# A streaming encoder step on one core: the projection stage gets its tokens already turned, and forms its halves between two chunks

## The reference, cut to what matters

```
h    = rmsnorm(x, ln1_g)                  # x: (tokens, 1024)
proj = h @ w_in                           # 1024 -> 3080 columns
xc   = causal_conv(x_lru, ..., lru_cw) + lru_cb     # 4 taps, out += xp[j:j+L] * w[j]
hs   = rglru(xc, ...);  out_a = hs * gelu(y_lru)
qkv_c = silu(causal_conv(qkv, ..., gdn_cw))
beta = sigmoid(b_logit);  g = -exp(alog) * softplus(a_logit + dtb)
```

## Time and profile before

| | |
|---|---|
| median of 3 runs | 3766.71 us (3763.04 to 3767.36) |
| the profiled execution's own time | 3768.46 us |
| its span, first to last instruction | 3766.8 us |
| TensorE busy over the span | 85% |
| VectorE busy | 57% |
| ScalarE busy | 41% |
| GpSimd busy | 22% |
| first matmul of group 0 / of the last group | 22.79 us / 1357.97 us |

### The profile page before, as it was taken

How to read it: one execution, slowest core, us unless ns; L and a number is a source line. 1 busy time by engine, 2 the same in 40 slices (tenths; PEclk the granted TensorE clock), 3 DMA queues, 4 the chain that set the end, 5 groups by cost and what they waited for, 6 DMA issues and landing times. The chain is left out here.

```text
span 3766.8 us, 66113 instructions
## 1 busy us (share of the span) xinstructions
PE 3191.2 (85%) x18658; PEld 1938.3 (51%) x18659; DVE 2155.4 (57%) x5335; ACT 1538.5 (41%) x3032; POOL 823.0 (22%) x1002
## 2 busy tenths in 40 slices
PE   8997979788797976699999999998499999999920
PEld 3443434333343456577777777766355555555500
DVE  6574757566665764477677777766433333333358
ACT  6464656556555662233333333332122222222222
POOL 0000000000000001255445554553111111111145
PEclk9998989899898985799999999999799999999965
DMA  4456656574747534445554455433367778985378
GB/s 144 142 182 224 213 194 231 184 258 164 274 159 243 190 127 144 121 138 148 145 146 129 130 145 149 131 112 92 132 223 252 269 266 283 324 295 185 110 275 333
DMA packets 487498, 716.00 MB, mean 190 GB/s; under 512 B 92272, under 2 KB 241360, under 8 KB 486992
## 3 DMA queue, kind: packets, MB, share of 16 engines
q1 hardware_dynamic: 404096, 480.63, 41.3%
q10 hardware_dynamic: 54288, 146.56, 9.8%
q0 software_dynamic: 28864, 86.09, 6.3%
HBM read 442.22 MB, written 270.92 MB: 189 GB/s over the span
## 5 line engine op out<-in xcount | busy, mean ns | idle before, releaser
L338 PE MATMUL pP<-h_hi,w_hi 128*128 128x512 f16 (+1 forms) x1728 | 639.0, 374 | 86.1 <-ACT win L430 67.1
L338 PE MATMUL pP<-h_lo,w_hi 128*128 128x512 f16 (+1 forms) x1728 | 637.6, 373 | 0.0
L338 PE MATMUL pP<-h_hi,w_lo 128*128 128x512 f16 (+1 forms) x1728 | 635.9, 372 | 0.0
L1863 PE MATMUL ebank<-w_halves,rowsT_hi 128*128 x1568 | 485.4, 381 | 1.5 <-ACT rowsT_hi L1899 0.9
L529 DVE SCALAR_TENSOR_TENSOR halves<-stage,halves 128x512 f16<-128x512 f32 x384 | 254.6, 687 | 200.6 <-ACT halves L400 200.4
L400 ACT ACTIVATE halves<-stage 128x512 f16<-128x512 f32 x384 | 236.4, 625 | 273.7 <-DMA stage<-in_raw 264.4
L569 DVE SCALAR_TENSOR_TENSOR cv<-win,cols_sb,cv 128x512 f32<-128x512 f32 (+1 forms) x432 | 305.5, 707 | 35.8 <-issue 1.4
L338 PEld LDWEIGHTS pP<-h_hi,w_hi 128*128 128x128 f16 x1728 | 174.6, 101 | 293.1 <-ACT win L430 80.4
L1863 PE MATMUL ebank<-w_halves,rowsT_lo 128*128 x784 | 298.9, 381 | 0.0
L298 POOL TENSOR_TENSOR ss<-ss,eps 128x4 f32<-128x4 f32 (+1 forms) x9 | 2.2, 249 | 1295.7 <-ACT junk L386 1295.7
L338 PEld LDWEIGHTS pP<-h_hi,w_lo 128*128 128x128 f16 x1728 | 175.1, 101 | 191.7 <-issue 18.3
(11 more groups left out here) (344 smaller groups left out, 6666.9 us busy)
## 6 DMA issues: line engine op xcount, KB each, us to landing
stage<-in_raw SPq DMA_DIRECT2D x384, 256.0 KB, 4.0
split<-halves SPq DMA_DIRECT2D x384, 256.0 KB, 3.3
w_halves<-split SPq DMA_DIRECT2D x32, 2048.0 KB, 11.6
y<-yb ACTq DMA_DIRECT2D x98, 512.0 KB, 7.4
ft<-mixin SPq DMA_DIRECT2D x33, 1280.0 KB, 8.5
mixin<-qo ACTq DMA_DIRECT2D x128, 256.0 KB, 3.7
w_halves<-split SPq DMA_DIRECT2D x32, 1024.0 KB, 6.1
xt<-in_x SPq DMA_DIRECT2D x33, 512.0 KB, 5.2
```

Source lines behind the costliest of these rows:

```text
L338: ins = nc.tensor.matmul(pP[n % NPB][:, 0:N], w[:, k, c0:c0 + P], h[:, k, 0:N], start=(k + i == 0), stop=(k == KD - 1 and i == 2))
L1863: ins = nc.tensor.matmul((M0, M1)[p][:, :], x[p][:, k, :], w[:, bass.ds(s, 1), k, half, :].rearrange("p a n -> p (a n)"), start=(k + i == ...
```

## The change

The tokens are also given with rows and columns exchanged (`xT`). SP loads eight blocks of 128 x 512 of it during the first chunks of the group before (steps "W"), 2 KB in a row; no transposes are left. The token tiles themselves are still loaded, for the sum of squares only, into `gy` (two at a time), and the four passes over them are spread over four steps "N". VectorE forms a diagonal of the inverse norms ("D"), TensorE spreads them over all partitions by one float32 matmul with ones ("E", behind chunk Q8), VectorE scales each block in place ("H", in the Z part), and ahead of Z3 ScalarE writes `h_hi` and VectorE `h_lo` of the next group ("T"), each block k as soon as Z3's matmuls have read it. The first chunk of a group waits for each block apart. The oldest convolution tap on VectorE goes; instead ScalarE writes the newest tap straight from the bank into `cv` by a second activation. There are four banks `pP` instead of three, and seven raw buffers instead of four; `carry_s` and `hl_s` now lie in `stage` and are loaded behind the last piece. `asq` and `amax` share other tiles.

```diff
-NRAW, NHALF = 4, 4
+NRAW, NHALF = 7, 4
...
     for m in range(3, QC):
-        out += [("Q", m)] + p() + [("S", m - 1)] + [("N", 0)] * (m == 6) + [("B", 0)] * (m == 9) + p(2)
-    out += [("Z", 0)] + p() + [("S", QC - 1)] + p(3) + [("Z", 1)] + p(4) + [("Z", 2)] + p(3) + [("Z", 3)] + p()
+        out += [("Q", m)] + p() + [("S", m - 1)] + [("N", m - 2)] * (m < 6) + [("D", 0)] * (m == 7) + [("E", 0)] * (m == 8)
+        out += [("B", 0)] * (m == 9) + p(2)
+    out += [("Z", 0)] + p(2) + [("S", QC - 1)] + p(3) + [("Z", 1)] + [("H", k) for k in range(4)] + p(3)
+    out += [("H", k) for k in range(4, KD)] + [("Z", 2)] + p(3) + [("T", k) for k in range(KD)] + [("Z", 3)] + p()
...
-    NPB = 3
+    NPB = 4
...
+            def spread(g, nt):
+                pe.wait_ge(*norm_did.at("D", g))
+                pe.wait_ge(*norm_did.at(f"H{KD - 1}", g, back=1))
+                nc.tensor.matmul(pR[:, 0:nt * P], ones[:, :], rg[:, 0:nt * P], start=True, stop=True
+                                 ).then_inc(*spread_did.did("E"))
...
-                        ins = nc.tensor.transpose(turned[k % 4][:, t * P:(t + 1) * P], xt[:, t, k * P:(k + 1) * P], ident)
-                    ins.then_inc(*pe_did.did(f"T{k}"))
-                pe.wait_ge(*dve_did.at(f"L{KD - 1}", g))
...
                         for k in range(KD):
+                            if n == 0:
+                                pe.wait_ge(*h_did.at(f"L{k}", g))
...
+            def high(k, g, nt):
+                act.wait_ge(*norm_did.at(f"H{k}", g))
+                act.wait_ge(*pe_did.at(f"{last}.{k}", g, back=1))
+                nc.scalar.activation(h_hi[:, k, 0:nt * P], xT[:, k, 0:nt * P], ACT.Copy).then_inc(*hi_did.did(f"T{k}"))
...
+                        nc.scalar.activation(window(c, 3, stream), shaped(made, stream), ACT.Copy, scale=PROJ)
+                        if 4 <= c < 8:
+                            act.wait_ge(*pe_did.at(f"G{c - 4}", g))
+                        nc.scalar.activation(cv[:, c % 4, 0:N], made, ACT.Identity, scale=col("cw", 4 * c + 3),
+                                             bias=col("cb", m) if kind == "X" else 0.0).then_inc(*act_did.did(f"{kind}{m}"))
...
+            def diagonal(g, nt):
                 dve.wait_ge(*rs_did.at("rs", g))
...
+            def scaled(k, g, nt):
...
+                nc.vector.scalar_tensor_tensor(xT[:, k, 0:N], xT[:, k, 0:N], ln16[:, k:k + 1], pR[:, 0:N],
+                                               ALU.mult, ALU.mult).then_inc(*norm_did.did(f"H{k}"))
...
-                        if kind == "X":
-                            nc.vector.tensor_scalar(dst, window(c, 0, stream), cw(0), col("cb", m), ALU.mult, ALU.add)
-                        else:
-                            nc.vector.tensor_scalar(dst, window(c, 0, stream), cw(0), None, ALU.mult)
                         nc.vector.tensor_copy(kept[:, c], new)
-                        for j in range(1, 4):
+                        for j in (2, 1, 0):
```

More of the change, by code:

```diff
@@ L243, in _ @@
                 if n == 6:
-                    load(1, GT)
+                    for k in range(KD):
+                        turned_load(k, 1, GT)
+                if 14 <= n < 14 + GT:
+                    token_load(n - 14, 1)
                 if n >= 2:
@@ L250, in raw, with group @@
                              ).then_inc(raw_in[i % NRAW], 16)
[L252 to L258, removed]
+            def group(g, base, count, following, n):
+                for kind, i in seq:
+                    if kind == "P" and i < count:
+                        sp.wait_ge(lo_done, base + i + 1)
+                        sp.dma_start(T["split"][bass.ds(base + i, 1)].rearrange("a p b n -> p (a b) n"),
+                                     halves[i % NHALF][:, :, :]).then_inc(halves_out[i % NHALF], 16)
+                        if i < following:
+                            raw(base + i + NRAW, i)
+                    elif kind == "W":
+                        turned_load(i, g + 1, n)
+                    elif kind == "R" and i == LC - 1:
+                        for t in range(min(2, n)):
+                            token_load(t, g + 1)
+                    elif kind == "N" and i + 2 < n:
+                        token_load(i + 2, g + 1)
             sp.wait_ge(w_split, len(wblocks))
@@ L262, in _ @@
                 raw(i, i)
[L263 to L266, removed]
+            with sp.Fori(1, groups - 1) as g:
+                group(g, (g - 1) * PER_GROUP, PER_GROUP, PER_GROUP, GT)
             rest = NE * PIECES - (groups - 2) * PER_GROUP
-            pieces((groups - 2) * PER_GROUP, rest, rest - NRAW)
+            group(groups - 1, (groups - 2) * PER_GROUP, rest, rest - NRAW, 1)
+            sp.dma_start(carry_s, T["conv_s"]).then_inc(states_in, 16)
+            sp.dma_start(hl_s, T["h_s"]).then_inc(states_in, 16)
             for n in range(NHALF):
@@ L360, in group @@
                         ins.then_inc(*pe_did.did("B0"))
[L362 to L365, removed]
+            spread(0, GT)
+            group(0, GT, GT, first=True)
+            with pe.Fori(1, groups - 1) as g:
+                group(g, GT, GT)
+            group(groups - 1, GT, 1)
+            group(groups, 1, 0)
         def shaped(ap, stream):
@@ L479, in _ @@
                 act.sem_inc(s, 16)
-            norm(0, GT)
-            act.wait_ge(setup_in, 16 * 4)
+            for t in range(GT):
+                act.drain()
+                act.wait_ge(first_in, 16 * GT)
+                norm(t, first_tiles[t], 0)
+            act.wait_ge(setup_in, 16 * 2)
             nc.scalar.activation(sp4[:, :], col("lam", 0, LC), ACT.Exp, scale=-1.0)
@@ L494, in _ @@
             act.drain()
+            newest = col("cw", 0, 4 * CC).rearrange("p (c j) -> p c j", j=4)[:, :, 3]
+            nc.scalar.activation(newest, newest, ACT.Copy, scale=PROJ)
+            act.drain()
             nc.scalar.copy(carry[:, 0, 0:1], sp4[:, 0:1]).then_inc(params, 1)
             split(0)
+            for k in range(KD):
+                high(k, 0, GT)
             split(1)
@@ L533, in group @@
                 N = nt * P
[L534 to L537, removed]
                 kept = carry_s if stream else carry
@@ L541, in group @@
                         split(block_of[kind, m] + 2)
-                    if kind == "N" and following:
-                        norm(g + 1, following)
+                    if kind == "D" and following:
+                        diagonal(g + 1, following)
+                    elif kind == "H" and following:
+                        scaled(m, g + 1, following)
+                    elif kind == "T" and following:
+                        low(m, g + 1, following)
                     elif kind == "P" and m < pieces:
@@ L621, in _ @@
             split(0)
+            for k in range(KD):
+                low(k, 0, GT)
             split(1)
```

172 lines of the change are left out of this document (95 added, 77 removed).

## The result

The changed kernel takes 3681.27 us (median of 4 runs, 3671.11 to 3684.69) against 3767.03 for the kernel before in the same runs: ratio 0.9769, 95% interval 0.9749 to 0.979. It is 85.8 us faster, where 148 were forecast (3619). The profiled execution took 3681.03 us, with a span of 3679.4.

What follows compares the result with a forecast made beforehand. The prediction took the Q and Z part as limited by latency first, then transfers. Six groups of 22.6 us plus 14 made 149.6 less than 3768.5, so 3619; own range 3585 to 3655 (0.55), 8 in 10 3550 to 3692.

Steps and rivals of the forecast that it cites:

- The boundary: Between groups: TensorE's 25.1 us to the next chunk would become about 1.3 if ScalarE and VectorE are in time.
- The Q and Z part: Behind chunk Q2 of each full group: 72 us of transfers (25.1 MB at 0.35 MB/us), plus 10 us of remaining stalls.
- I leave half, 10 us: Q and Z part: of 19 us per group above transfers and norm's stop, 10 stay, from the ring of four halves.
- seven buffers remove what is load latency: Q and Z part: seven raw buffers remove the load latency among 19 us per group; the ring of four halves stays.
- 2 us lost out of the 10: Behind chunk Q8: TensorE waits up to 16 us for VectorE's diagonal, but only 2 us per group are lost.
- seven loads can land meanwhile: At step B, where ScalarE stops for its tables and VectorE waits 4.9 us: seven raw loads can land during the stop.
- The norm's stop: Step N: ScalarE's four passes, GpSimd's power and VectorE's scaling stop the pieces about 9.5 us per group; this goes wholly.
- Group 7: The group with 48 pieces: 148.95 us to about 140, -9, from its boundary and waits behind `win`.
- I take nothing: Work shifted between engines: ScalarE 98 to 107 us per group, VectorE 110 to 106; counted as no effect, bounds -3 and +4.
- the halves ring: Rival, chance 0.21: four halves buffers and stores behind loads keep nearly the old pace; 162 us per group, 3692.
- TensorE's pace: Rival, chance 0.17: lateness vanishes and TensorE sets the pace; groups take 137 to 141 us, time 3549.
- Stores behind loads: Rival, chance 0.04: on SP's shared queue stores land in 7.5 us or more instead of 3.3; slower, 3826.

Runs made afterwards that it cites:

- experiment 10: The changed kernel, but the first chunk of a group waits for the last lo half instead of for each block; 3708.39 us, ratio 0.9865 to the kernel before.
- experiment 4: The changed kernel with six pieces per group moved forward, behind Y0, X0 and Y1 instead of behind Q6 to Q11; 3646.81 us.
- experiment 1: The changed kernel with four raw buffers instead of seven, halves staying at four; 3693.82 us.
- experiment 3: The changed kernel with step E behind chunk Q11 instead of behind Q8; 3646.80 us.
- experiment 7: The changed kernel with E behind Q11, six pieces per group moved forward, and step B behind Y1 instead of behind Q9; 3583.18 us.
- experiment 12: The kernel before, with VectorE's share of the norm two chunks later, behind Q8, ScalarE's passes unmoved; 3746.64 us, ratio 0.9962.
- experiment 6: The changed kernel with the convolution as before: four taps on VectorE, one evacuation on ScalarE; 3673.48 us, ratio 0.9768 to the kernel before.
- experiment 11: The changed kernel with three banks instead of four for the chunks; 3669.37 us, ratio 0.9765 to the kernel before.
- experiment 2: The changed kernel with four raw buffers and seven halves instead of seven and four; 3692.13 us.
- 8: The kernel before, with six pieces per group moved forward, behind Y0, X0 and Y1 instead of behind Q6 to Q11; 3719.00 us, ratio 0.9884.

## Why the forecast had the sign and the mechanism, and missed the size

The boundary. Forecast 1.3 us plus lateness, a wait of up to 12; measured 8.35 in group 3. That the first chunk is released block by block, and not by the last lo half, is worth 34 us alone (experiment 10), the largest single piece of the gain that was isolated. This step was right. What leaving out the transposes gives, apart from that, was not tried alone.

The start and the last group were right within 1 us in their sums; their parts weren't taken apart.

The Q and Z part failed, in a term that was mis-sized. The opening part came as forecast (64.6 + 2.6 = 67.2; 67.0 in the mean of the six groups of the trace). The rest was forecast at 72 + 10 + 1.3 = 83.3 us and took 91.0 in the mean. By the forecast's own split, "I leave half, 10 us" should have been 157.9 - 64.6 - 2.6 - 1.3 - 72 = 17.4. The windows of group 3 show a second way to read it: the 72 was the term that was too small. The forecast counted the 39 pieces, 14 outputs and two token tiles that the list has behind Q3, 25.1 MB. But ScalarE, VectorE and SP reach them later than TensorE does, and while TensorE is between Q3 and the next group, 28.4 MB pass. In group 3 43 loads are issued there, and this much else:

```profile
stage<-in_raw SPq DMA_DIRECT2D x43, 256.0 KB, 4.6
mixin<-qo ACTq DMA_DIRECT2D x15, 256.0 KB, 4.6
gy<-in_x SPq DMA_DIRECT2D x4, 512.0 KB, 5.5
mixin<-oa ACTq DMA_DIRECT2D x2, 256.0 KB, 5.2
```

At the forecast's 0.35 MB/us, which the window bears out (307 / 0.88 = 349 GB/s), these are 81 us, and DMA stands 10 to 11 us, about what had been left with the boundary. So the stalls came out right in their sum, by luck, for their parts were wrong; and the trace before had 24 of them, not 28.6. That the bytes are not the whole of it either shows in experiment 4. The parts:

- "seven buffers remove what is load latency", some 9 us of 19: three more raw buffers gave 2.5 per group (experiment 1). The wait for loads became a smaller one for stores (20.1 us against 38.9 in group 3; 100 against 119 in five groups for seven and four raw buffers). The forecast had itself reckoned 1.6 us per piece before, and 1.5 as what the transfers ask: that leaves 4 us over 39 pieces, and it took 9.
- E, "2 us lost out of the 10": the wait itself was foreseen (up to 16 us; 10.4), but its place cost 3 to 4 per group (experiment 3). The reason given for the small cost was that ScalarE and VectorE would have Q8 to work on meanwhile. They had, and then stood 3.2 and 3.7 us (604.26 in VectorE's timeline) for Q9, which TensorE ended late because of the wait and the lower clock behind it. The forecast had put this passing on at 2.
- B, "seven loads can land meanwhile": this was put at nothing, and moving B gave 3 per group (experiment 7). With ScalarE and VectorE at a stand no halves are made that could be stored, and DMA fell to 0.13.
- The norm's stop, "about 9.5 goes wholly": of VectorE's share, 4.5, only 2 to 2.5 showed (experiment 12). How much ScalarE's spread passes brought is open.

These are single effects, each measured in one surrounding, and needn't add up.

Group 7 gained 3.2 us instead of 9, and group 0 4.5 instead of 7. The waits at their ends did go: the next group's first matmul starts 0.22 us behind the last in both. But E's wait (6.03 us in group 7, 1.7 in group 0) took part of it, and the forecast had reckoned none for these two. With E later they are 5.5 and 3.5 us shorter (experiment 3).

"I take nothing" for the engines' shifted work was right in the sum (experiment 6). The fourth bank, which was to cover wobbles, is not needed (experiment 11).

Of the rivals, the halves ring came nearest in time (3692 against 3681), nearer than the forecast itself, and its sign, waits for the store of halves, is there. But experiment 2 says that the name of the ring is not the cause: with the rings exchanged the raw loads hold instead. What counts more is the number of pieces and stops behind Q3 (experiments 4, 7 and 8). TensorE's pace, the rival of 3549, was nearly reached once these were removed (3574, full groups of 142 where it said 137 to 141). Stores behind loads: their landing grew from 3.3 us to 4.1 in group 3,

```profile
split<-halves SPq DMA_DIRECT2D x57, 256.0 KB, 4.1
stage<-in_raw SPq DMA_DIRECT2D x56, 256.0 KB, 4.4
```

far from the 7.5 at which it would have decided.

## What to carry to other kernels

When work is crowded into one part of a loop, count it per part, not per turn: six of 56 pieces moved to the opening part, where DMA stood more than half the time, gave half as much as the whole change, and needed no new buffer. Count it by where each engine is and not by where the list has it: transfers listed ahead of a point are still running when the fastest engine passes it. A wait put into the engine that runs ahead is not free because that engine has time: those behind it use up what it had made ready and then stand, and it restarts at the lower clock; put such a step where its input is long done. Three more buffers in one of two rings of equal size moved most of the wait to the other ring here; look at both before crediting the latency. Where one engine's output is the next turn's input, release it block by block: what was lost at the turn wasn't caught up here.

## What the runs showed of the hardware

With loads and stores of 256 KB, most of them on one queue, DMA was busy at a share of 0.99 or more in 54 windows of 5 us of groups 1 to 6; they moved 323 to 411 GB/s. Over the whole part behind Q3 a busy microsecond of DMA moved 0.34 MB before and 0.35 after, which is the forecast's rate. The forecast said that no window shows the 425 GB/s of the Trainium skill (HBM Reference, "Specifications (TRN2)") and that the full ones have 338 to 375. These were two windows; others of the same trace go further, up to

```profile
320.00:325.00 5.00, 1.06 (x10) 0.82 (x8) 2.49 (x4) 2.22 (x4) 0.00 (x0) 1.00 1.05 394
```

and after, the best window is within 4% of the page's figure:

```profile
1040.00:1045.00 5.00, 5.00 (x24) 2.25 (x23) 3.60 (x7) 3.15 (x7) 0.00 (x0) 1.00 1.06 411
```

So single windows come near it, and the mean of this mixed traffic stays well below.

The same code behind the projection took 2330 to 2342 us in fourteen profiled executions, one of each kernel. A difference of 9 us between two traces of this kernel can be that alone, which is more than the 0.2% that the forecast took for the limit.
